# Hybrid block with 32 experts on one core: first weight piece cast by GpSimd in three transfers, scatter between gate and up, last product in bank 6

## The chip, the core and the metric

The kernel runs on one core of a Trainium2 chip. The core has TensorE (PE, with its weight loads as PEld), VectorE (DVE), ScalarE (ACT), GpSimd (POOL), SyncE (SP), which here does nothing but issue transfers, and 16 DMA engines. The metric is the device time of one execution in microseconds (us), lower is better.

## The reference, cut to what matters

One decoder block in float32 for 256 tokens of width 1024: a mixing part (window attention and a short convolution), then a mixture of 32 experts of which each token uses four. All 32 experts are computed, and each has three matrices of 1024 x 1024, so that 96 matrices of 4 MB (4.19 million bytes) must be read from HBM.

```
h = rms_norm(x, g_mix);  proj = h @ w_in + b_in
...
x = x + (sigmoid(ga) * y_attn + sigmoid(gc) * y_conv) @ w_out
h = rms_norm(x, g_ffn)
top_logit, top_idx = lax.top_k(h @ w_router + b_router, 4);  top_w = softmax(top_logit)
for each expert e, for the tokens sent to it:
    g = min(xb @ w_gate[e] + b_gate[e], 7);  u = clip(xb @ w_up[e] + b_up[e], -7, 7)
    y = (g * sigmoid(1.702 * g) * (u + 1)) @ w_down[e] + b_down[e]
    x[token] += top_w * y
out = rms_norm(x, g_final)
```

## The kernel before

The order of the work is written out by hand, engine by engine; semaphores join the engines, and nothing is scheduled by a planner.

**The first stage** (to about 250 us) is the mixing part. A float32 product is made there from a high part and a low rest: weights come in pieces of 128 x 2048 elements into one of three raw slots, a cast rounds them to the high part `wH`, and a subtraction gives the rest `wL`. The very first piece is special: `x` and the piece are the first transfers on SP's queue (line 344 and 347), the piece in two halves with the semaphores `first_in` and `piece_full[0]`. ScalarE casts its first quarter (`first_weights(0, 2)`, line 1045), VectorE the second (line 1297), GpSimd the second half (line 1662). Meanwhile PE runs `WARM` = 3 idle products on zeros (line 610, two instructions of the hardware for one), then transposes the normed `x` (line 587; VectorE makes it in eight quarter rows at line 1287); ScalarE and VectorE turn the transposes into `hH` and `hL` (lines 1049 and 1299), and PE starts `project_first` (line 600).

**The second stage** is the experts. An expert `j` has two slots ("runs") of 2 MB for gate, up and down each. All are streamed by SP through a ring of ten slots, in the order of use; from expert 5 on in whole matrices (lines 474 to 479, only the up matrix of every fifth expert in two parts), in the last two experts by slots (line 361). SP waits until PE has used the slot (`weights_used`) before it issues the next load into it. The last four slots (`HALVED`: LAST - 3 to LAST) land in two halves each, the very last in a half and two quarters (line 375).

PE does for each expert: the gate product (`wide(4, ...)`, line 831, bank 4, bias at line 797), the up product (bank 5), then `scatter(j, j)` (line 845), which adds the output of the expert before to the 256 tokens in banks 0 to 3, then `turn_act` (line 858) and `turn_weights` (line 852, into bank 4), then `gather(j + 1)` (line 761, bank 6), which fetches the next expert's tokens, and the down product (bank 7) with `turn_xe` (line 769) between its two slots. The down product waits for `aT_ready`, which ScalarE gives after copying the turned activations (`take_act`, line 1175). ScalarE also copies the gathered rows (`take_rows`, line 1143) and the finished output (`take_y`, line 1180), and VectorE does `swiglu`, `take_weights` (`S_ready`, line 1532) and `take_xe` (`xe_ready`, line 1545).

The experts 0 to 4 are written out, 5 to 29 are a loop over groups of five (`UNROLL`), and `last_pair` does 30 and 31 in an order of its own: gate 30, gather, up 30, `turn_xe`, scatter, the turns, gate 31, up 31, down 30, scatter, down 31, and a last scatter. Both down products there write bank 7, so that the scatter of 30 stands between them and waits for ScalarE's copy. The final norm and the output follow.

Of the kernel before, what the change touches and what calls it, by code (L numbers as in the profile page):

```python
# [27 lines left out]
P = 128  # L28
# [33 lines left out]
UNROLL = 5  # L62
FREED = (0, 1, 4)
LAST = NE * EP - 1
HALVED = (EP, *(RING + p for p in FREED), LAST - 3, LAST - 2, LAST - 1, LAST)
SSQ0 = 2 + 2 * NKV
RSTD0 = 4
WARM = 3
# [60 lines left out]
def hybrid_block(nc, A, out):  # L129
    ctx = ExitStack()  # L130
    with ctx:
# [128 lines left out]
        first_in, second_high, rest_high = sem("first_in"), sem("second_high"), sem("rest_high")  # L260
# [77 lines left out]
        def _(sp):  # L338
# [6 lines left out]
            for half, full in enumerate((first_in, piece_full[0])):  # L345
                ks = slice(4 * half, 4 * half + 4)
                sp.dma_start(raw_slot(0).rearrange("p (k n) -> p k n", k=KB)[:, ks],
                             w_in[:, ks, KCOL * PW:(KCOL + 1) * PW]).then_inc(full, 16)
# [164 lines left out]
        def _(pe):  # L513
# [286 lines left out]
            def wide(b, src, first_p, uses, bias_of, base=None, between=None, paired=False, by_halves=None):  # L800
# [3 lines left out]
                for run in range(RUNS):  # L804
# [14 lines left out]
                    for k2 in range(RUN):  # L819
                        if halved and base + p == LAST and k2 == RUN // 2:  # L820
                            pe.wait_ge(quarter_full, 16)
                        elif halved and k2 == (RUN - 1 if base + p == LAST else RUN // 2):
                            pe.wait_ge(slot_full[s], uses(p))
# [15 lines left out]
            def scatter(nth, chunk):  # L839
# [3 lines left out]
                for t in range(TT):  # L843
# [5 lines left out]
            def turn_weights(j):  # L849
                pe.wait_ge(Gw_ready, j + 1)  # L850
                for t in range(TT):
                    tr = pe.transpose(bank(4, t * P, P), Gw[:, t, :, :].rearrange("p h c -> p (h c)"), ident)  # L852
# [27 lines left out]
            def expert(j, c, uses, paired, up_halves):  # L880
# [26 lines left out]
                if not at(j, 0):  # L907
# [15 lines left out]
            def group(it, paired):  # L923
                for c in range(UNROLL):
                    expert(it * UNROLL + c, c, lambda p: (it - paired) * (16 * in_group) + 16 * (p // RING + 1), paired,
                           it * 16 if paired else None)

            def last_pair():
# [73 lines left out]
        def _(act_e):  # L1002
# [41 lines left out]
            act_e.wait_ge(first_in, 16)  # L1044
            nc.scalar.copy(*first_weights(0, 2)).then_inc(first_high, 1)
# [132 lines left out]
            def take_y(used):  # L1178
                act_e.wait_ge(weights_used, used)
                nc.scalar.copy(ysb, psum[:, 7, :]).then_inc(ysb_ready, 1)  # L1180
# [11 lines left out]
            for j in range(UNROLL):  # L1192
# [7 lines left out]
            with act_e.Fori(1, NE // UNROLL) as it:  # L1200
# [13 lines left out]
            take_y(NE * EP)  # L1214
# [23 lines left out]
        def _(dve):  # L1238
# [291 lines left out]
            def take_weights(j):  # L1530
                dve.wait_ge(S_turned, j + 1)
                v.tensor_copy(S, psum[:, 4, 0:256]).then_inc(S_ready, 1)  # L1532
# [39 lines left out]
            for j, used in ((NE - 2, (NE - 2) * EP), (NE - 1, (NE - 2) * EP + 2 * RUNS)):  # L1572
# [70 lines left out]
        def _(pool):  # L1643
# [16 lines left out]

            pool.wait_ge(piece_full[0], 16)
# [63 lines left out]
```

## Time and profile before

| what | us |
|---|---|
| median of 3 runs | 1163.14 (1162.24 to 1163.76) |
| the profiled execution, its own time | 1162.93 |
| its span in the profile | 1161.1 |
| PE busy in it | 1120.4 (97%) |
| 16 DMA engines busy, main queue | 92.9% of the span |

The profile's times count from the start of the span; 1.8 us of the execution lie around it. A busy PE includes modelled ends of pipelined products; a row's mean is the time of one instruction from its start to that end, so that steps are better read from starts.

### The profile page before, as it was taken

The page shows a single profiled execution, that of the slowest core. Times are in us where ns is not written, and L with a number is a line of the kernel's source. Part 1 is how long each engine was busy: PE and PEld are TensorE (multiplying, and loading weights), DVE is VectorE, ACT ScalarE, POOL GpSimd, SP SyncE. Part 2 cuts the span into 40 slices and gives each one's busy share as a digit, 9 for nine tenths or more (in the row PEclk, how much of TensorE's full clock was granted, in tenths as well). Part 3 has the DMA queues.
Part 4 walks back from the last instruction along what each step waited for, and adds up shares of the span by engine and source line. Part 5 has one row for each costly group of instructions (what it writes and reads, how often), then busy time and mean ns, then how long its engine had stood idle before and what let it go on. Part 6 is the DMA issues. An engine that isn't in the chain of part 4 may idle for free.

```text
span 1161.1 us, 14240 instructions
## 1 busy us (share of the span) xinstructions
PE 1120.4 (97%) x5623; PEld 522.9 (45%) x5623; DVE 359.9 (31%) x684; ACT 238.9 (21%) x426; POOL 26.9 (2%) x59
## 2 busy tenths in 40 slices
PE   8999999999999999999999999999999999999997
PEld 7888888973333333333333333333333333333332
DVE  6988897742111112112111111111111111111111
ACT  6676765421000000100010000000000000000002
POOL 2100000000000000000000000000000000000000
PEclk9999999999999999999999999999999999999999
DMA  9455749899999999999999999999999999999996
GB/s 295 157 175 169 263 143 350 298 407 428 428 427 434 427 430 432 427 432 430 430 432 430 435 433 432 432 426 433 429 432 433 427 437 433 432 430 424 430 423 244
DMA packets 62913, 447.44 MB, mean 385 GB/s; under 512 B 4649, under 2 KB 44933, under 8 KB 46501
## 3 DMA queue, kind: packets, MB, share of 16 engines
q1 hardware_dynamic: 62608, 446.93, 92.9%
q8 instruction: 20, 0.33, 0.1%
q10 hardware_dynamic: 277, 0.12, 0.0%
q14 instruction: 8, 0.07, 0.0%
HBM read 445.59 MB, written 1.05 MB: 385 GB/s over the span
## 4 chain that ended last, share of the span: by engine, by line
PE 75%; DMA 23%; ACT 0%; DVE 0%; issue 0%; POOL 0%; ACTq 0%; DVEq 0%; POOLq 0%
PE psum L831 42%; DMA ring<-in_w_up 20%; PE psum L540 10%; PE psum L544 5%; PE psum L845 4%; PE psum L761 4%; DMA ring<-in_w_down 3%; PE psum L560 2%; PE psum L769 1%; PE psum L858 1%; PE psum L797 1%; PE psum L610 0%; PE psum L852 0%; PE psum L600 0%; PE psum L526 0%; PE psum L874 0%
## 5 line engine op out<-in xcount | busy, mean ns | idle before, releaser
L831 PE MATMUL psum<-ring,work 128*64 128x512 f32 x3072 | 693.1, 601 | 27.0 <-DMA ring<-in_w_up 21.6
L831 PEld LDWEIGHTS psum<-ring,work 128*64 128x64 f32 x3072 | 217.6, 138 | 453.6 <-issue 406.0
L1522 DVE TENSOR_SCALAR work<-psum 128x512 f32<-128x512 f32 x32 | 22.1, 692 | 285.2 <-PE psum L831 285.2
L540 PE MATMUL psum<-hh,w 128*128 128x512 f32 x384 | 97.4, 395 | 0.0
L1266 DVE TENSOR_TENSOR w<-ring,w 128x1024 fp32r<-128x1024 f32 x74 | 90.4, 1264 | 8.6 <-ACT w L1015 8.3
L1527 DVE TENSOR_SCALAR work<-psum 128x512 f32<-128x512 f32 x32 | 22.1, 692 | 196.4 <-PE psum L831 196.4
L1175 ACT COPY work<-psum 128x512 f32<-128x512 f32 x32 | 18.8, 587 | 301.9 <-PE psum L858 301.8
L1015 ACT CAST w<-ring 128x1024 fp32r<-128x1024 f32 x74 | 74.2, 1049 | 28.3 <-PE psum L544 15.2
L1545 DVE TENSOR_TENSOR work<-psum,g2k 128x256 f32<-128x256 f32 x62 | 23.4, 419 | 168.7 <-PE psum L769 168.7
L540 PEld LDWEIGHTS psum<-hh,w 128*128 128x128 f32 x384 | 68.9, 189 | 15.0 <-ACT w L1015 1.3
L1184 ACT ACTIVATE work<-work 128x512 f32<-128x512 f32 x32 | 20.1, 630 | 230.4 <-DVE work L1522 230.4
L1180 ACT COPY work<-psum 128x512 f32<-128x512 f32 x32 | 18.8, 586 | 228.2 <-PE psum L831 228.2
L845 PE MATMUL psum<-work 64*128 64x512 f32 x256 | 63.6, 615 | 1.4 <-ACT work L1180 1.4
L761 PE MATMUL psum<-xres,work 128*64 128x512 f32 x248 | 61.5, 618 | 0.0
L544 PEld LDWEIGHTS psum<-hh,w 128*128 128x128 f32 x384 | 52.3, 190 | 3.8
L544 PE MATMUL psum<-hh,w 128*128 128x256 f32 x384 | 53.5, 282 | 0.0
L845 PEld LDWEIGHTS psum<-work 64*128 64x128 f32 x256 | 22.0, 186 | 41.9 <-issue 38.6
L1532 DVE COPY work<-psum 128x256 f32<-128x256 f32 x32 | 13.6, 425 | 56.2 <-PE psum L852 47.1
L1525 DVE TENSOR_TENSOR work<-work 128x512 f32<-128x512 f32 x32 | 22.2, 693 | 25.8 <-ACT work L1184 25.8
L1143 ACT COPY work<-psum 128x512 f32<-128x512 f32 x31 | 18.2, 586 | 52.4 <-PE psum L761 52.4
L858 PEld LDWEIGHTS psum<-cst,work 128*128 128x128 f32 x128 | 17.9, 209 | 24.4 <-DVE work L1528 22.0
L769 PEld LDWEIGHTS psum<-cst,work 128*128 128x128 f32 x124 | 17.3, 209 | 25.2 <-issue 25.2
(210 smaller groups left out, 688.5 us busy)
## 6 DMA issues: line engine op xcount, KB each, us to landing
ring<-in_w_gate SPq DMA_DIRECT2D x25, 4096.0 KB, 39.5
ring<-in_w_down SPq DMA_DIRECT2D x25, 4096.0 KB, 39.7
ring<-in_w_up SPq DMA_DIRECT2D x20, 4096.0 KB, 37.1
ring<-in_w_up SPq DMA_DIRECT2D x23, 2048.0 KB, 35.5
ring<-in_w_gate SPq DMA_DIRECT2D x13, 2048.0 KB, 13.1
ring<-in_w_in SPq DMA_DIRECT2D x25, 1024.0 KB, 5.1
ring<-in_w_down SPq DMA_DIRECT2D x8, 2048.0 KB, 13.3
ring<-in_w_down SPq DMA_DIRECT2D x10, 1024.0 KB, 37.4
```

The lines of the kernel that those rows point to most:

```text
L540: pe.matmul(bank(b[m]).rearrange("p (x t) -> p x t", x=2), wH[:, par, m, k, :], both[:, :, k, :], start=(k == 0), stop=(k == KB - 1))
L544: mm = pe.matmul(bank(b[m], 0, T), wL[:, par, m, k, :], both[:, 0, k, :], start=False, stop=(k == KB - 1), skip_group_check=True)
L560: mm = pe.matmul(bank(b[t], t * PW, PW).rearrange("p (m n) -> p m n", m=2), x[:, k, t * P:(t + 1) * P], w[:, par, :, k, :], start=(k == 0 ...
L761: mm = pe.matmul(psum[64 * h:64 * h + 64, 6, :].rearrange("p (i r) -> p i r", r=RUN), Gr[:, t, :], x_runs[:, :, h, :], start=(t == 0), sto ...
L769: tr = pe.transpose(bank(6, r * P, P), rows.rearrange("p (i r) -> p i r", r=RUN)[:, :, r], ident)
L831: mm = pe.matmul(to, src[:, k, :], moving, start=(bias_of is None and k == 0), stop=(k == KB - 1), tile_position=(0, 64 * h))
L845: pe.matmul(bank(2 * t + h), S[64 * h:64 * h + 64, t * P:(t + 1) * P], ysb[64 * h:64 * h + 64, :], start=False, stop=False, skip_group_che ...
L858: tr = pe.transpose(bank(5, b * P, P), act_runs[:, b // RUN, :, b % RUN], ident)
L1015: nc.scalar.copy(wH[:, par, m, :, :], raw_slot(s).rearrange("p (k n) -> p k n", k=KB)[:, :, m * P:(m + 1) * P],).then_inc(wH_ready, rise i ...
L1266: v.tensor_tensor(wL[:, par, m, :, :], raw_slot(s).rearrange("p (k n) -> p k n", k=KB)[:, :, m * P:(m + 1) * P], wH[:, par, m, :, :].bitca ...
L1525: steps.link(v.tensor_tensor(gm, gm, sg, ALU.mult))
L1545: ins = v.tensor_tensor(to, turned, gain.unsqueeze(2).broadcast_to([P, RUN, CW]), ALU.mult)
```

## The change

Three edits. First, the first weight piece comes in three transfers (a quarter, a quarter, a half), all three parts are cast by GpSimd, and `WARM` is 2. Second, from expert 10 on (`BACKLOG` = 2 groups of five are written out now) PE scatters the expert before between the gate and the up product, and gathers for the next one ahead of the turns; ScalarE copies the gathered rows ahead of the activations. Third, in the last pair: VectorE takes the next expert's tokens ahead of the scatter weights, which stand in bank 7 instead of 4 for expert 30; the wait on `S_ready` moves from ahead of gate 31 to ahead of down 30; the last down product writes bank 6 and has the scatter of expert 30 in its middle; and slot LAST - 4 lands in halves too.

```diff
+BACKLOG = 2
-HALVED = (EP, *(RING + p for p in FREED), LAST - 3, LAST - 2, LAST - 1, LAST)
+HALVED = (EP, *(RING + p for p in FREED), LAST - 4, LAST - 3, LAST - 2, LAST - 1, LAST)
-WARM = 3
+WARM = 2
@@ sync
-            for half, full in enumerate((first_in, piece_full[0])):
-                ks = slice(4 * half, 4 * half + 4)
+            for k0, k1, full in ((0, 2, first_in), (2, 4, second_in), (4, KB, piece_full[0])):
+                ks = slice(k0, k1)
@@ tensor, wide()
                     for k2 in range(RUN):
+                        if middle is not None and run == 0 and k2 == RUN // 2:
+                            middle()
@@ tensor, expert()
+                if caught_up:
+                    scatter(j, j)
                 wide(5, xe, c * EP + RUNS, uses, 1, base, None, paired, up_halves if c == UNROLL - 1 else None)
                 if at(j, 0):
                     pe.wait_ge(wT_ready, 1)
+                if at(j, 0) or caught_up:
                     gather(j + 1)
                 else:
                     scatter(j, j)
...
-                if not at(j, 0):
+                if not (at(j, 0) or caught_up):
                     gather(j + 1)
@@ tensor, last_pair()
-                turn_weights(a)
+                turn_weights(a, 7)
                 pe.wait_ge(xe_ready, b + 1)
                 pe.wait_ge(picked, b + 1)
-                pe.wait_ge(S_ready, b)
                 wide(4, xe, 2 * RUNS, uses, 0, base)
...
+                pe.wait_ge(S_ready, b)
                 wide(7, aT, 4 * RUNS, uses, None, base, turn_last)
-                scatter(b, b)
                 pe.wait_ge(aT_ready, b + 1)
-                wide(7, aT_last, 5 * RUNS, uses, None, base)
-            group(0, False)
-            with pe.Fori(1, NE // UNROLL) as it:
-                group(it, True)
+                wide(6, aT_last, 5 * RUNS, uses, None, base, middle=lambda: scatter(b, b))
+            for it in range(BACKLOG):
+                group(it, it > 0, False)
+            with pe.Fori(BACKLOG, NE // UNROLL) as it:
+                group(it, True, True)
@@ scalar
-            act_e.wait_ge(first_in, 16)
-            nc.scalar.copy(*first_weights(0, 2)).then_inc(first_high, 1)
...
+                    take_rows(j + 1)
                     take_act(j)
-                    take_rows(j + 1)
...
-            take_y(NE * EP)
+            act_e.wait_ge(scattered, 4 * NE)
+            take_y(NE * EP, 6)
@@ vector
-                if k == 2:
-                    dve.wait_ge(first_in, 16)
-                    v.tensor_copy(*first_weights(2, 4)).then_inc(second_high, 1)
...
-                if j == NE - 1:
-                    dve.wait_ge(scattered, 4 * NE)
-                take_weights(j)
                 if j < NE - 1:
                     take_xe(j + 1)
+                    take_weights(j, 7)
+                else:
+                    dve.wait_ge(scattered, 4 * NE)
+                    take_weights(j)
@@ gpsimd
+            pool.wait_ge(first_in, 16)
+            g.tensor_copy(*first_weights(0, 2)).then_inc(first_high, 1)
+            pool.wait_ge(second_in, 16)
+            g.tensor_copy(*first_weights(2, 4)).then_inc(second_high, 1)
             pool.wait_ge(piece_full[0], 16)
             g.tensor_copy(*first_weights(4, 8)).then_inc(rest_high, 1)
```

PE's program for one expert of the loop, before; L797 is the bias, L831 the products (16 stand for one matrix), L845 the scatter, L858 and L852 the turns of activations and weights, L761 the gather, L769 the turn of the next tokens:

```order
L797 MATMUL psum<-bias,chosen 64x512 x2
L831 MATMUL psum<-ring,work 64x512 x16
L797 MATMUL psum<-bias,chosen 64x512 x2
L831 MATMUL psum<-ring,work 64x512 x16
L845 MATMUL psum<-work 128x512 x4
L858 MATMUL psum<-cst,work 128x128 x4
L852 MATMUL psum<-cst,work 128x128 x2
L757 REGISTER_ALU
L761 MATMUL psum<-xres,work 64x512 x4
L831 MATMUL psum<-ring,work 64x512 x8
L769 MATMUL psum<-cst,work 128x128 x4
L831 MATMUL psum<-ring,work 64x512 x8
```

And in the changed kernel, where the line numbers are up to 3 higher (L834 products, L848 scatter, L861 and L855 turns, L762 gather):

```order
L798 MATMUL psum<-bias,chosen 64x512 x2
L834 MATMUL psum<-ring,work 64x512 x16
L848 MATMUL psum<-work 128x512 x4
L798 MATMUL psum<-bias,chosen 64x512 x2
L834 MATMUL psum<-ring,work 64x512 x16
L758 REGISTER_ALU
L762 MATMUL psum<-xres,work 64x512 x4
L861 MATMUL psum<-cst,work 128x128 x4
L855 MATMUL psum<-cst,work 128x128 x2
L834 MATMUL psum<-ring,work 64x512 x8
L770 MATMUL psum<-cst,work 128x128 x4
L834 MATMUL psum<-ring,work 64x512 x8
```

The scatter moved ahead of the up product's bias, and the gather took its place ahead of the turns; between the turns and the down product nothing is left.

PE's program at the end of the last pair before, from the bias of gate 31 on:

```order
L797 MATMUL psum<-bias,chosen 64x512 x2
L831 MATMUL psum<-ring,work 64x512 x16
L797 MATMUL psum<-bias,chosen 64x512 x2
L831 MATMUL psum<-ring,work 64x512 x24
L858 MATMUL psum<-cst,work 128x128 x4
L852 MATMUL psum<-cst,work 128x128 x2
L831 MATMUL psum<-ring,work 64x512 x8
L845 MATMUL psum<-work 128x512 x4
L831 MATMUL psum<-ring,work 64x512 x16
L845 MATMUL psum<-work 128x512 x4
```

And in the changed kernel:

```order
L798 MATMUL psum<-bias,chosen 64x512 x2
L834 MATMUL psum<-ring,work 64x512 x16
L798 MATMUL psum<-bias,chosen 64x512 x2
L834 MATMUL psum<-ring,work 64x512 x24
L861 MATMUL psum<-cst,work 128x128 x4
L855 MATMUL psum<-cst,work 128x128 x2
L834 MATMUL psum<-ring,work 64x512 x12
L848 MATMUL psum<-work 128x512 x4
L834 MATMUL psum<-ring,work 64x512 x12
L848 MATMUL psum<-work 128x512 x4
```

The first of the two scatters moved four products back, into the middle of the first slot of the last down product.

## Rows read from the trace of the kernel before

**Rows 1.** The page: PE's share of the span; the DMA engines' busy tenths in 40 slices.

```profile
PE 1120.4 (97%) x5623; PEld 522.9 (45%) x5623; DVE 359.9 (31%) x684; ACT 238.9 (21%) x426; POOL 26.9 (2%) x59
...
DMA  9455749899999999999999999999999999999996
```

**Rows 2.** Stretches: length, busy us of PE PEld DVE ACT POOL, granted clock, DMA share, GB/s.

```profile
16.50:244.00 227.50, 227.50 (x1453) 201.20 (x1452) 184.99 (x268) 143.82 (x262) 10.47 (x13) 1.00 0.69 235
500.00:630.00 130.00, 130.00 (x618) 46.31 (x614) 22.82 (x49) 11.95 (x20) 1.17 (x5) 1.00 1.00 432
634.00:1050.00 416.00, 390.81 (x1798) 135.50 (x1794) 69.39 (x155) 34.19 (x58) 3.28 (x14) 0.98 1.00 432
1051.30:1060.10 8.80, 8.73 (x34) 2.63 (x34) 0.00 (x0) 0.00 (x0) 0.00 (x0) 0.81 0.99 425
```

**Rows 3.** Chain that ended last: start us, length us, what; the last DMA in it.

```profile
1014.30 37.03 DMA ring<-in_w_up
```

**Rows 4.** Three of the last loads, each: issue (ns, us) and us to landing.

```profile
L375 SPq DMA_DIRECT2D ring<-in_w_down x1: 2062/2062/2062, 1099.8 to 1099.8; - x1
...
DMA to landing us min/median/max: 39.5/39.5/39.5
...
L375 SPq DMA_DIRECT2D ring<-in_w_down x1: 12155/12155/12155, 1103.2 to 1103.2; - x1
...
DMA to landing us min/median/max: 41.1/41.1/41.1
...
L375 SPq DMA_DIRECT2D ring<-in_w_down x1: 3321/3321/3321, 1124.0 to 1124.0; - x1
...
DMA to landing us min/median/max: 25.8/25.8/25.8
```

**Rows 5.** Timeline of the last experts: start us, length us, instruction, idle before.

```profile
1051.37 8.78 PE L831 MATMUL psum<-ring,work 128*64 128x512 f32 x32 [2.36 <-DMA ring<-in_w_up]
...
1086.66 1.99 PE L845 MATMUL psum<-work 64*128 64x512 f32 x8
...
1088.58 0.75 PE L858 MATMUL psum<-cst,work 128*128 128x128 f32 x4
...
1089.36 0.59 ACT L1175 COPY work<-psum 128x512 f32<-128x512 f32 x1 [8.33 <-PE psum L858]
...
1089.47 1.94 PE L761 MATMUL psum<-xres,work 128*64 128x512 f32 x8
...
1119.70 0.42 PE L797 MATMUL psum<-bias,chosen 96*64 96x512 bf16 x2 [1.18 <-DVE work L1545]
...
1142.68 1.99 PE L845 MATMUL psum<-work 64*128 64x512 f32 x8 [0.69 <-ACT work L1180]
...
1144.60 7.09 PE L831 MATMUL psum<-ring,work 128*64 128x512 f32 x32
```

**Rows 6.** Timeline of the first microseconds.

```profile
2.63 5.30 PE L610 MATMUL psum<-ring 128*128 128x512 f32 x6 [2.63 <-POOL ring L1646]
...
8.01 1.97 PE L587 MATMUL psum<-cst,normed 128*128 128x128 f32 x16
...
8.20 1.13 DVE L1287 TENSOR_SCALAR normed<-xres,small 128x256 f32<-128x256 f32 x4
...
9.32 3.03 ACT L1049 ACTIVATE hh<-psum,parT 128x256 fp32r<-128x256 f32 x8 [0.75 <-PE psum L587]
...
9.49 1.04 POOL L1662 CAST w<-ring 128x1024 fp32r<-128x1024 f32 x1 [1.48 <-DMA ring<-in_w_in]
...
10.50 4.22 PE L600 MATMUL psum<-hh,w 128*128 128x256 f32 x32 [0.45 <-issue]
...
11.04 2.44 DVE L1299 SCALAR_TENSOR_TENSOR hh<-psum,parT,hh 128x256 fp32r<-128x256 f32 x6
```

**Rows 7.** Groups by form: busy us, mean ns; the idle products and the same shape later.

```profile
L610 PE MATMUL psum<-ring 128*128 128x512 f32 x6 | 5.3, 1054 | 2.6 <-POOL ring L1646 2.6
...
L743 PE MATMUL psum<-xres,cst 128*128 128x512 f32 x8 | 3.9, 616 | 0.0
```

More of the change, by code:

```diff
@@ L259, in hybrid_block @@
         quarter_full, quarter_used = sem("quarter_full"), sem("quarter_used")
-        first_in, second_high, rest_high = sem("first_in"), sem("second_high"), sem("rest_high")
+        first_in, second_in, second_high, rest_high = sem("first_in"), sem("second_in"), sem("second_high"), sem("rest_high")
         x_in = [sem(f"x_in{t}") for t in range(TT)]
@@ L798, in add_bias, with wide @@
                               columns(bias3[:, bias_of, :], h), start=True, stop=False, tile_position=(0, 64 * h))
-            def wide(b, src, first_p, uses, bias_of, base=None, between=None, paired=False, by_halves=None):
+            def wide(b, src, first_p, uses, bias_of, base=None, between=None, paired=False, by_halves=None, middle=None):
                 if bias_of is not None and not (base == 0 and first_p == 0):
@@ L837, in wide, with scatter @@
                     mm.then_inc(weights_used, 1)
-            def scatter(nth, chunk):
+            def scatter(nth, chunk, ts=range(TT)):
                 pe.wait_ge(ysb_ready, chunk)
                 pe.wait_ge(S_ready, chunk)
-                for t in range(TT):
+                for t in ts:
                     for h in range(2):
@@ L847, in scatter, with turn_weights @@
                                   tile_position=(64 * h, 0)).then_inc(scattered, 1)
-            def turn_weights(j):
+            def turn_weights(j, b=4):
                 pe.wait_ge(Gw_ready, j + 1)
                 for t in range(TT):
-                    tr = pe.transpose(bank(4, t * P, P), Gw[:, t, :, :].rearrange("p h c -> p (h c)"), ident)
+                    tr = pe.transpose(bank(b, t * P, P), Gw[:, t, :, :].rearrange("p h c -> p (h c)"), ident)
                 tr.then_inc(S_turned, 1)
@@ L878, in at, with expert @@
                 return isinstance(j, int) and j == n
-            def expert(j, c, uses, paired, up_halves):
+            def expert(j, c, uses, paired, up_halves, caught_up):
                 base = (j - c) * EP if isinstance(j, int) else None
@@ L921, in _, with group @@
             in_group = UNROLL * EP // RING
-            def group(it, paired):
+            def group(it, paired, caught_up):
                 for c in range(UNROLL):
                     expert(it * UNROLL + c, c, lambda p: (it - paired) * (16 * in_group) + 16 * (p // RING + 1), paired,
-                           it * 16 if paired else None)
+                           it * 16 if paired else None, caught_up)
             def last_pair():
@@ L1176, in take_act, with take_y @@
                                psum[:, 5, :].rearrange("p (b h c) -> p b h c", b=4, h=2)).then_inc(aT_ready, 1)
-            def take_y(used):
+            def take_y(used, b=7):
                 act_e.wait_ge(weights_used, used)
-                nc.scalar.copy(ysb, psum[:, 7, :]).then_inc(ysb_ready, 1)
+                nc.scalar.copy(ysb, psum[:, b, :]).then_inc(ysb_ready, 1)
             def squash(j):
@@ L1191, in _ @@
             nc.scalar.copy(wT[:, :], psum[0:NE, 6, 0:256]).then_inc(wT_ready, 1)
-            for j in range(UNROLL):
+            for j in range(BACKLOG * UNROLL):
                 squash(j)
@@ L1199, in _ @@
                 take_y((j + 1) * EP)
-            with act_e.Fori(1, NE // UNROLL) as it:
+            with act_e.Fori(BACKLOG, NE // UNROLL) as it:
                 for c in range(UNROLL):
@@ L1528, in swiglu, with take_weights @@
                 v.scalar_tensor_tensor(act, uc, 1.0, gm, ALU.add, ALU.mult).then_inc(act_ready, 1)
-            def take_weights(j):
+            def take_weights(j, b=4):
                 dve.wait_ge(S_turned, j + 1)
-                v.tensor_copy(S, psum[:, 4, 0:256]).then_inc(S_ready, 1)
+                v.tensor_copy(S, psum[:, b, 0:256]).then_inc(S_ready, 1)
             def gained(hs):
```

## The prediction

> **What bounds the kernel now.** I began with the page. PE is busy for 97% of the span, which looks like a kernel bound by PE; but the DMA engines, too, stand at nine tenths from slice 10 on [rows 1]. So two engines are near their limits, and the stretches say which one gives the time. From 500 to 630 us PE passes 618 products without idling; an expert of this order has 126 (96 of weights, 8 scatter, 8 gather, 4 bias, 10 turns), so it takes 126 x 130 / 618 = 26.5 us [rows 2]. From 634 to 1050 us it passes 1798 in 416 us, 29.15 us an expert, and idles for 25 us, while the transfers run at 432 GB/s and a DMA share of 1.00 in both stretches [rows 2]. One matrix is 4.19 MB, so it lands every 9.71 us and three take 29.1 us: from about 630 us on the weights set the pace. Before that PE was slower than it could be only because the ring still held a stock, which it ate up at 2.6 us an expert.
>
> Two things follow. The transfers are saturated from about slice 8 on, so nothing that PE does in the middle moves their end; it moves only if the whole stream starts earlier. And what remains is the end, after the last time that PE waited for a transfer. The chain gives it: an up matrix issued at 1014.30 lands 37.03 us later, at 1051.33 [rows 3]. From there PE works without another wait for weights to 1144.60 + 7.09 = 1151.69, the end of the last product, which is 9.4 us ahead of the span's end; of other waits in that time there are 1.18 and 0.69 us [rows 5]. Did PE then fall behind the transfers? The last quarter of the last slot is issued at 1124.0 and lands after 25.8 us, at 1149.8 [rows 4]. PE takes the last two slots from 1144.60, so 3.43 us each to the next start, and comes to that quarter three quarters into the second slot, at 1150.7. So PE is later than the weights by 0.9 us and no more. That is the most that a better order of PE can give there, unless the stream itself comes earlier.
>
> **The change part by part, by the chain's end first: the scatter between gate and up.** In the changed rows an expert has the same instructions; what is new is which of them lie ahead of a wait. For experts 10 to about 14, where PE sets its own pace, the order costs something. The scatter (1.92 us from its start at 1086.66 to the next at 1088.58) used to cover VectorE's work behind the up product; the gather (1.77 us to the next start) takes that place and covers it about as well. But the gather used to cover ScalarE's copy of the turned activations, too. That copy starts at 1089.36, 0.78 us behind the turns, and takes 0.59 [rows 5], so it is ready 1.4 us behind their start, while the two turns take 0.89 (1088.58 to 1089.47) [rows 5]. So PE now waits 0.5 to 0.55 us ahead of each down product. ScalarE's new order (rows first) does not add to it, since its 0.6 us copy of the rows runs beside the turns. At 26.5 + 0.55 = 27.1 us PE is still faster than the transfers' 29.1, so it only meets them later, and the stream doesn't notice: cost nothing, because the 2 us an expert that it lacks to the pace of the transfers cover it.
>
> From about 650 us on, PE used to idle at up matrices and then scatter; now it scatters first. At the wait at 1051.37 it had idled for 2.36 us, and the two slots behind it took 8.78 us [rows 5] where 6.9 are usual, with a granted clock of 0.81 in that stretch [rows 2], that is part of it at the lower of the two levels, 1.2 GHz. The wait becomes shorter by the 1.92 us of the scatter, some 0.5 us remain, and the 1.9 us of slow clock should go too. From 1051.4 on I step PE through, with each matrix landing 9.71 us after the one before:
> - up 28 ends at 1058.3, gather and turns and the wait to 1061.5, down to 1069.2 (before: 1072.4). Then gate 29 waits for its landing at 1051.3 + 19.4 = 1070.8.
> - gate 29 to 1077.7, scatter, up 29 (1.9 + 0.2 + 6.9) to 1086.7, gather to 1088.5. Down 29 lands at 1090.2 and PE starts it there; before it started at 1089.47 + 1.77 = 1091.2.
>
> So of 3.2 us that the new order wins after the last wait, 0.9 are left two matrices later: the weights are in the way again. **The last pair:** up 30 ends 0.9 us earlier, and gate 31, which waited 1.18 us for `take_xe` [rows 5], no longer does. In its place comes `picked`, GpSimd's choice of the bias, which I put at 0.3 us of wait. Gate 31 then starts 1.8 us earlier, at 1118.1, and up 31 at 1125.2, both a little behind their landings. Then the pieces of 1 MB: the second half of down 30's second slot lands at 1099.8 + 39.5 = 1139.3 and the second half of down 31's first at 1103.2 + 41.1 = 1144.3 [rows 4], the ones around them 2.5 us apart. PE takes the former's 8 products from 1139.4 to 1141.1, waits for the first half of down 31 (1141.8), works to 1143.6, scatters for 1.9, then does one slot and a half: 1145.5 + 1.7 + 3.4 = 1150.7. The copy of bank 7, for which the scatter waited 0.69 us [rows 5], lies under the half slot. The last product ends at 1150.9 against 1151.7: **-0.8 us**. Splitting slot LAST - 4 lets up 31 pass that slot without a wait (its first half lands 2.5 us sooner); nothing is on the path for it.
>
> **The head.** The idle products end at 2.63 + 5.30 = 7.93 and the transposes start at 8.01 [rows 6]; with two instead of three the idle ones end at 6.2. But then VectorE is in the way: it makes the second token tile's quarters from 8.20 on, 0.28 us each [rows 6], and ScalarE's first `hH`, which needs the transpose of the first of them, starts at 9.32. That quarter is ready at about 8.5, its transpose was the ninth of sixteen, at 8.01 + 8 x 0.11 = 8.9. Now it can follow at 8.55. So the chain to PE's first product (10.50 [rows 6]) moves by 0.35 to 0.45 us. VectorE loses its cast (0.42 us), but it lay in a gap: the six products that follow it start at 11.04 [rows 6] because `hH` was not there yet. GpSimd has the two new casts, half of 1.04 us each [rows 6], between 8.05 and 9.3, and the third starts at 9.49 as before, because its data comes then. Everything that PE needs is cast a microsecond ahead. The third transfer costs SP 0.5 us more issue time, while its engines are busy with what is queued (the piece needed next comes by bandwidth, not by issue). From 16.5 to 244 us PE is busy for all of 227.5 us [rows 2], so the shift reaches the point where SP gets ring slots, and with it the stream: **-0.4 us** for all that follows.
>
> What speaks against this: VectorE's eight quarters (0.28 us for 256 columns each [rows 6]) now lie beside GpSimd's casts. If each cast held VectorE up for its 0.52 us, the second tile's first quarter would come at 9.0 instead of 8.5, `hH` at 9.4 instead of 9.32, and the head would win nothing or lose 0.1. No row shows such a block, so I keep -0.4 and take that for a rival. The Trainium skill, "SBUF — State Buffer", section "Who interferes with whom", states it as a rule: VectorE in a two-port mode and GpSimd hold one pair of ports exclusively, and the other blocks for the whole instruction. By that rule the sum would lose its -0.4.
>
> Sum on the profiled execution: 1162.93 - 0.8 - 0.4 = 1161.7. Its time lies 0.2 under the median of the three runs, so by that median 1163.14 - 1.2 = **1161.9 us**, 0.10% less. A measurement of this kernel tells no less than about 0.2%, 2.3 us, from no change.
>
> **The rivals.**
> - *The head gives nothing*, because the casts hold VectorE up as priced above, or by the clock. The idle products take 5.3 / 6 = 0.88 us each, the same shape later 3.9 / 8 = 0.49 [rows 7]: they run at the low level of 1.2 GHz, and the transposes behind them, 0.11 us apart, no longer. With one less and an idle half microsecond ahead of the first transposes the higher clock may come later. The stretch at 1051 us lost 8.78 - 6.9 = 1.9 us to it [rows 5]; the same here gives -1.2 + 1.9 = +0.7. So 1162.3 to 1163.9. The Trainium skill, "TensorE: Matmul & The Clock Gate", part 1, says that the throttled state is the default and that activity releases it, which fits that row. Chance 0.16.
> - *PE wins its full idle product* (1.77 us) at the head, because the quarters are not what holds it. The stream moves with it, and the end by at most 0.9 more: 1163.1 - 2.7 = 1160.4. Against it stands the start of the quarters at 8.20 after the first tile's. Chance 0.07.
> - *The wait ahead of the down product becomes the bound*, on the other side. It decides from 29.15 - 26.5 = 2.6 us an expert. If turns, both copies and VectorE's work stood one behind the other (0.7 + 0.6 + 0.6 + 1.4 = 3.3 us), an expert would take 29.8 us, twenty of them from 520 us on would end at 1116 instead of 1099, and the time would be 1180. The rows show the copies beside PE's work, not behind it [rows 5]. Chance 0.03.
> - *The new order wins nothing at the end*: PE's lead is used up between the landings, because the last pieces come some tenths later than I read them or a turn or a `picked` waits longer than I put it; the 0.8 us are only the difference of two such chains. Then -0.4 alone is left, 1162.7. Chance 0.12.
>
> **How the numbers follow.** The forecast, 1161.2 to 1162.6, has 0.57; 0.05 is left for what I don't see, half on each side. The range that holds 8 in 10 reaches from between the second rival and the forecast to the top of the first, 1160.6 to 1163.9. Faster by over 0.2% needs 1160.8 or less: the second rival, the lower edge of the forecast and the unseen, 0.11. Slower by over 0.2% needs 1165.5: the third rival and the unseen, 0.06. The rest, 0.83, is no change.
>
> **What would show it.** The first `hH` near 8.95 and PE's first product near 10.1; two idle products and transposes 0.11 us apart. In the loop a wait of 0.5 us ahead of each down product, released by ScalarE; waits for up matrices under 1 us where 2.36 were, and no granted clock under 1 there. Landings still 9.71 us apart, the last near 1149.4. The last product's end near 1150.5, with its last wait for a weight quarter. I would be wrong if the rate of the transfers changed, since 1% of it is 9 us, or if the stream had gaps behind the first experts that the earlier start closes or opens.

## The result, and the profile after

| | median us | runs |
|---|---|---|
| before | 1162.36 (1161.36 to 1164.53) | 22 |
| changed kernel | 1164.27 (1162.78 to 1168.41) | 22 |

The ratio is 1.0019, with a 95% interval of 1.0013 to 1.0024: the change costs 2.2 us (1.5 to 2.8). The forecast was 1161.9, and 1164.27 lies above the top of the range, 1163.9. The forecast stood on the median of three runs, 1163.14, which is 0.8 us above the median of 22; as a difference, -1.2 was forecast and +2.2 came. The profiled execution took 1165.37 us, with a span of 1163.2 (before 1162.93 and 1161.1).

The page of the changed kernel, for [rows 1], and its stretches, for the third of [rows 2]:

```profile
PE 1118.3 (96%) x5621; PEld 520.8 (45%) x5621; DVE 360.9 (31%) x683; ACT 238.0 (20%) x425; POOL 27.9 (2%) x61
...
DMA  9455749899999999999999999999999999999996
...
q8 instruction: 25, 0.41, 0.1%
...
634.00:1050.00 416.00, 390.74 (x1820) 134.67 (x1818) 70.42 (x160) 33.99 (x57) 3.26 (x14) 1.00 1.00 432
```

PE is busy 2.1 us less and its clock is full in the long stretch, where it was 0.98; the transfers run at the same 432 GB/s. PE gained, and the span grew nonetheless. One row differs, the loads of instructions: 25 here, and in the page of before 20:

```profile
q8 instruction: 20, 0.33, 0.1%
```

The timeline of the first microseconds, for [rows 6]:

```profile
8.56 0.63 POOL L1665 CAST w<-ring 128x512 fp32r<-128x512 f32 x1
...
8.79 2.46 DVE L1292 TENSOR_SCALAR normed<-xres,small 128x256 f32<-128x256 f32 x4
9.14 0.67 POOL L1667 CAST w<-ring 128x512 fp32r<-128x512 f32 x1
...
10.21 3.02 ACT L1053 ACTIVATE hh<-psum,parT 128x256 fp32r<-128x256 f32 x8 [3.41 <-PE psum L588]
...
11.05 0.70 PE L588 MATMUL psum<-cst,normed 128*128 128x128 f32 x4 [0.30 <-DVE normed L1292]
...
11.75 2.03 PE L601 MATMUL psum<-hh,w 128*128 128x256 f32 x15
```

VectorE's four quarters beside the casts take 2.46 us where they took 1.13, and PE's first product starts at 11.75 instead of 10.50. (0.6 us of that was there before the casts, at the quarters' start of 8.79 against 8.20; where the quarters start differs from execution to execution, so the length is the reading.)

The last experts on PE, for [rows 5]:

```profile
1043.92 7.09 PE L834 MATMUL psum<-ring,work 128*64 128x512 f32 x32 [1.12 <-DMA ring<-in_w_gate]
...
1053.63 7.09 PE L834 MATMUL psum<-ring,work 128*64 128x512 f32 x32 [0.37 <-DMA ring<-in_w_up]
...
1063.79 3.65 PE L834 MATMUL psum<-ring,work 128*64 128x512 f32 x16 [0.46 <-ACT work L1179]
...
1120.29 0.42 PE L798 MATMUL psum<-bias,chosen 96*64 96x512 bf16 x2 [0.32 <-POOL chosen L1693]
...
1144.41 1.94 PE L834 MATMUL psum<-ring,work 128*64 128x512 f32 x8 [0.64 <-DMA ring<-in_w_down]
1146.28 1.99 PE L848 MATMUL psum<-work 64*128 64x512 f32 x8
1148.20 5.57 PE L834 MATMUL psum<-ring,work 128*64 128x512 f32 x24
1154.51 1.99 PE L848 MATMUL psum<-work 64*128 64x512 f32 x8 [0.74 <-ACT work L1184]
```

The waits are about those that were forecast: 0.46 ahead of the down product, 0.37 for the up matrix where 2.36 was, 0.32 for `picked`. Yet the last product ends at 1148.20 + 5.57 = 1153.77 instead of 1151.69. The landings say why. The last two quarters of the weights, with their time from issue to landing:

```profile
L376 SPq DMA_DIRECT2D ring<-in_w_down x2: 2106/2122/2137, 1124.8 to 1126.9; - x2
...
DMA to landing us min/median/max: 25.6/26.1/26.5
```

The last lands 25.6 us behind 1126.9, at 1152.6; before it was 1149.8 [rows 4]. So the end of the stream moved by 2.8 us, and PE follows it more closely (1.2 us instead of 1.9). The stream's beginning moved by 1.1 of these: the first expert's up matrix is issued at 215.5 here and lands 7.5 us later, at 223.1, and landed at 222.0 before. The other 1.7 us arise within the stream, where I had said that nothing could.

### The profile page after: what moved, and what is told of

It reads as the page before. It is cut to its first block, busy times and chain, and to the rows that moved or that the text cites. A ratio compares the mean times of both kernels' runs of the same rounds, so it can differ in the third digit from the quotient of the medians.

```text
span 1163.2 us, 14215 instructions
## 1 busy us (share of the span) xinstructions
PE 1118.3 (96%) x5621; PEld 520.8 (45%) x5621; DVE 360.9 (31%) x683; ACT 238.0 (20%) x425; POOL 27.9 (2%) x61
## 4 chain that ended last, share of the span: by engine, by line
PE 63%; DMA 35%; ACT 1%; DVE 0%; issue 0%; ACTq 0%; POOL 0%; SPq 0%; DVEq 0%
PE psum L834 34%; DMA ring<-in_w_down 13%; DMA ring<-in_w_gate 11%; DMA ring<-in_w_up 10%; PE psum L541 10%; PE psum L545 5%; PE psum L762 3%; PE psum L848 3%; PE psum L561 2%; PE psum L770 1%; PE psum L861 1%; PE psum L798 1%; DMA cst<-in_constants 0%; PE psum L877 0%; PE psum L601 0%; PE psum L527 0%
## 5 line engine op out<-in xcount | busy, mean ns | idle before, releaser
L834 PE MATMUL psum<-ring,work 128*64 128x512 f32 x3072 | 685.9, 595 | 31.7 <-DMA ring<-in_w_gate 15.5
L834 PEld LDWEIGHTS psum<-ring,work 128*64 128x64 f32 x3072 | 213.9, 137 | 439.5 <-issue 380.6
L848 PE MATMUL psum<-work 64*128 64x512 f32 x256 | 63.6, 615 | 0.7 <-ACT work L1184 0.7
L762 PE MATMUL psum<-xres,work 128*64 128x512 f32 x248 | 60.6, 611 | 0.0
L848 PEld LDWEIGHTS psum<-work 64*128 64x128 f32 x256 | 22.0, 186 | 41.2 <-issue 39.4
L762 PEld LDWEIGHTS psum<-xres,work 128*64 128x64 f32 x248 | 17.2, 139 | 32.7 <-issue 32.7
L861 PEld LDWEIGHTS psum<-cst,work 128*128 128x128 f32 x128 | 18.0, 209 | 25.9 <-DVE work L1530 23.1
```

Of the source, the lines that this page charges most:

```text
L762: mm = pe.matmul(psum[64 * h:64 * h + 64, 6, :].rearrange("p (i r) -> p i r", r=RUN), Gr[:, t, :], x_runs[:, :, h, :], start=(t == 0), sto ...
L834: mm = pe.matmul(to, src[:, k, :], moving, start=(bias_of is None and k == 0), stop=(k == KB - 1), tile_position=(0, 64 * h))
L848: pe.matmul(bank(2 * t + h), S[64 * h:64 * h + 64, t * P:(t + 1) * P], ysb[64 * h:64 * h + 64, :], start=False, stop=False, skip_group_che ...
L861: tr = pe.transpose(bank(5, b * P, P), act_runs[:, b // RUN, :, b % RUN], ident)
```

## The experiments

Each kernel was timed in 11 runs, beside 33 of the kernel before that the kernels of one series share. An interval is about 0.09% wide on either side, 1.0 us, so that a single part of the change stands at the edge of what can be told; a difference given in us is the ratio's. A profile shows one execution.

**Series 1: the head and the order apart.** `e1_head_all` is the whole head of the change (three transfers, casts by GpSimd, two idle products) with the old order; `e2_casts` has the transfers and the casts with three idle products; `e3_warm2` has the two idle products alone; `e4_order` is the changed kernel with the head of before.

```diff
# e1, e2 (e1 also WARM = 2)
+            pool.wait_ge(first_in, 16)
+            g.tensor_copy(*first_weights(0, 2)).then_inc(first_high, 1)
+            pool.wait_ge(second_in, 16)
+            g.tensor_copy(*first_weights(2, 4)).then_inc(second_high, 1)
# e1, e2: the casts of ScalarE and VectorE go, the third transfer is that of e16
# e3
-WARM = 3
+WARM = 2
# e4: the change without these, ScalarE and VectorE cast as before
```

> The kernel before with all of the head of the change (three transfers, all casts on GpSimd, two idle products), order untouched. Theory 1, the head costs the time: the profile of the changed kernel has PE's first product at 11.75 instead of 10.50 us and all landings about 1.1 us later, so +1.0 to +1.3 us. Rival, the head is neutral and the order behind it costs the 2 us: within 0.3 us of before.

Measured: 1163.11 against 1161.98, ratio 1.0014 (1.0004 to 1.0023), +1.6 us.

> The kernel before with three transfers and all casts on GpSimd, but three idle products. Theory 1a, GpSimd's casts hold VectorE up: the second tile's four quarter rows take 2.4 us instead of 1.13 and the time is +0.6 to +1.2 us. Rival 1b, the missing idle product costs the time by a later clock: the quarters take 1.1 us and the time is -0.4 to +0.1.

Measured: 1162.87, ratio 1.0008 (0.9999 to 1.0017), +0.9 us.

> The kernel before with two idle products and nothing else. Theory 1a: transposes start near 7.0 us, the first product moves by -0.3 to 0 us, so the time is -0.3 to +0.1. Rival 1b: the granted clock rises only near 11 us, the transposes stand 0.2 us apart and the time is +0.5 to +1.0.

Measured: 1162.35, ratio 1.0001 (0.9992 to 1.0010).

> The changed kernel with the head of before (two transfers, casts on three engines, three idle products). If the head is the only loss, the order keeps what the prediction gave it at the end, -0.8 us to before. If the order itself has a price (the stream of weights is delayed in the middle, where the changed profile shows landings another 1.2 us later than the head explains), +0.5 to +1.2 us.

Measured: 1162.96, ratio 1.0006 (0.9997 to 1.0015), +0.7 us. The timeline of the head of `e2_casts`:

```profile
7.88 0.63 POOL L1657 CAST w<-ring 128x512 fp32r<-128x512 f32 x1
...
8.11 2.48 DVE L1285 TENSOR_SCALAR normed<-xres,small 128x256 f32<-128x256 f32 x4
8.45 0.67 POOL L1659 CAST w<-ring 128x512 fp32r<-128x512 f32 x1
...
9.40 1.04 POOL L1661 CAST w<-ring 128x1024 fp32r<-128x1024 f32 x1 [0.27 <-DMA ring<-in_w_in]
...
10.51 3.21 DVE L1294 SCALAR_TENSOR_TENSOR hh<-psum,parT,hh 128x256 fp32r<-128x256 f32 x8
...
11.08 2.75 PE L600 MATMUL psum<-hh,w 128*128 128x256 f32 x21
```

The four quarters start in time, at 8.11, and are stretched by 1.35 us. The second and the fourth of them by themselves, where 0.35 us is the length of one that nothing disturbs:

```profile
8.57 0.70 DVE L1285 TENSOR_SCALAR normed<-xres,small 128x256 f32<-128x256 f32 x1
...
9.45 1.13 DVE L1285 TENSOR_SCALAR normed<-xres,small 128x256 f32<-128x256 f32 x1
```

The second ends at 9.27, 0.15 us behind the end of the second cast (9.12), and the fourth at 10.58, 0.14 behind the end of the third (10.44). So the two new casts hold VectorE up for 0.2 and 0.35 us, and that is enough for the last quarter to meet the third cast, the half piece that GpSimd had before too: it costs the most, 0.78 us. In the kernel before, that cast started at 9.49, when the quarters were through. `hL` on the same engine (line 1294) then starts only at 10.51, and PE's first product waits for that. So by `e1_head_all` the head costs 1.6 us (0.5 to 2.7); the casts alone point the same way, but their interval reaches zero. In the times of `e3_warm2` the idle product shows no cost, and in its trace PE's first product starts 2.2 us behind the start of the second tile's quarters, where 2.3 were before. The order, which was to win 0.8, shows no gain either and points the other way.

**Series 2: what of the order costs.** `e5_written_out` only writes experts 5 to 9 out, in the old order; `e6_pair` has only the new last pair; `e7_loop` has the new order in the loop with the old pair and head; `e8_late_bias` is `e4_order` with PE's spreading of the down bias (the `spread_down_bias` call) moved from expert 4 to expert 9, away from the point near 397 us where SP issues late.

```diff
# e5 (PE; ScalarE's loop likewise)
+            for it in range(BACKLOG):          # BACKLOG = 2
+                group(it, it > 0, False)
+            with pe.Fori(BACKLOG, NE // UNROLL) as it:
+                group(it, True, False)
# e6: BACKLOG = 1, nothing caught up, the new last_pair
# e7: group(it, True, True) in the loop, the old last_pair
# e8
-                if at(j, UNROLL - 1):
+                if at(j, 2 * UNROLL - 1):
                     spread_down_bias()
```

> The kernel before, with the experts 5 to 9 written out on PE and ScalarE instead of looped and nothing else; the order of every engine's work stays as it was. Theory 2a, the order's loss is the price of more program: five more 16 KB code loads lie beside the weights, each keeps one DMA engine for about 1 us, and the stream is up to 1 us longer: +0.3 to +1.0 us. Rival 2b, it comes from the order itself: within 0.3 us of before.

Measured: 1163.22 against 1162.02, ratio 1.0010 (1.0001 to 1.0019), +1.2 us.

> The kernel before with the last pair of the change alone (bank 6, scatter in the middle, bank 7 for the weights, LAST - 4 in halves); loop order and head of before. The prediction's step for the end: gate 31 no longer waits 1.18 us, the second scatter no longer 0.69, and PE's last product ends 0.6 to 0.9 us nearer the last landing (1.89 us behind it before), so -0.5 to -0.9 us. Rival: the stream's own end moves later as in the two profiles with this tail, where one 1 MB piece took 3.3 to 3.5 us instead of 2.5, and the time is within 0.3 us of before.

Measured: 1161.97, ratio 1.0000 (0.9991 to 1.0009).

> The changed kernel's loop order (written-out experts 5 to 9, scatter between gate and up from expert 10 on) with the head and the last pair of before. Theory 2a: the reorder wins nothing where the stream sets the pace and the code loads remain, +0.2 to +1.0 us. Rival 2b, the new wait ahead of each down product costs at the end: more than +1 us. By the prediction's sum the end is the last pair's, so -0.3 to 0.

Measured: 1163.04, ratio 1.0007 (0.9998 to 1.0016), +0.8 us.

> The kernel of e4 (order and last pair of the change, head of before), with the down bias (8 products of 32 rows, 3.6 us, followed by the low clock at 383 us) moved from expert 4 to expert 9. Theory 3, the stream has one tight place: at about 397 us SP issues a matrix only 1.9 to 5.4 us ahead of the end of the one in flight, and when PE is late there the stream stops for 0.2 to 1.8 us. With the bias later that issue comes 5 us earlier, the stretch of three matrices takes 29.1 us in every profile, and the time is 0.4 to 1.0 us below e4's. Rival: the stream never stops there and the time is e4's within 0.3 us.

Measured: 1162.45, ratio 1.0004 (0.9995 to 1.0013), +0.5 us, which can't be told from the +0.7 of `e4_order`. The kernel with nothing new but five experts written out is as slow as the whole order: it executes the same instructions on the same data. What differs is where its code comes from. Transfers from 520 to 1100 us, of the kernel before, the changed one, and, from series 3, the one with ten experts more written out:

```profile
q1 hardware_dynamic: 9357, 250.16, 100.3%
```

```profile
q1 hardware_dynamic: 9309, 250.01, 100.3%
q8 instruction: 5, 0.08, 0.1%
```

```profile
q1 hardware_dynamic: 9336, 249.71, 100.2%
q8 instruction: 10, 0.16, 0.1%
```

In this stretch the kernel before, whose loop is running, loads no code, and each expert more that is written out brings one load of 16 KB (0.08 MB in five) into a stream that fills the engines.

**Series 3: the two suspects undone.** `e9b_order_looped` is `e4_order` with `BACKLOG` = 1 (the new order already from expert 5, no more code than before); `e10b_written_more` is `e5_written_out` with 3; `e11b_head_wait` is `e1_head_all` with GpSimd's casts kept behind VectorE's quarters; `e12b_all_mended` is the changed kernel with both mends.

```diff
# e9b, e12b
-BACKLOG = 2
+BACKLOG = 1
# e10b
-BACKLOG = 2
+BACKLOG = 3
# e11b, e12b
+            pool.wait_ge(normed_ready, 4 * TT)
             pool.wait_ge(first_in, 16)
             g.tensor_copy(*first_weights(0, 2)).then_inc(first_high, 1)
```

> The kernel of e4 (order and last pair of the change, head of before) with the experts 5 to 9 in the loop again, in the new order too (BACKLOG = 1). Theory 4, what the order costs is the written-out program: 20 code loads instead of 25, the stream from its first expert landing to its last back from 928.8 to about 927.4 us, and the time 0.8 to 1.5 us below e4's, so -0.8 to -0.2 against before. Rival 4b, the order of the work costs it: e4's time within 0.3 us.

Measured: 1162.23 against 1162.24, ratio 0.9999 (0.9990 to 1.0009).

> The kernel of e5 (order of before) with the experts 10 to 14 written out as well, so 30 code loads. Theory 4a, each load costs alike: another +0.8 to +1.3 us, +2.0 to +2.5 against before. Theory 4b, loads cost only where they meet an engine that is late already: anything from +1.2 to +2.5. Rival, the number of loads is not the cause: within 0.3 us of e5, or of before.

Measured: 1163.90, ratio 1.0014 (1.0005 to 1.0023), +1.6 us.

> The kernel of e1 (whole head of the change, order of before), with GpSimd's first cast waiting until VectorE has made all eight quarter rows. Theory 1a, the casts held VectorE up: the second tile's quarters take 1.13 us again instead of 2.47, ScalarE starts on hH near 8.9, PE's first product comes near 10.2 instead of 10.8 and the time is 0.6 to 1.6 us below e1's, so -0.4 to +0.4 against before. Rival, the third transfer or the later clock is what costs: e1's time within 0.3 us.

Measured: 1162.56, ratio 1.0002 (0.9993 to 1.0011), +0.2 us where `e1_head_all` had +1.6.

> The changed kernel with both mendings: GpSimd's casts wait for VectorE's quarters, and the experts 5 to 9 are in the loop (BACKLOG = 1). If the causes are the two that I hold them for, the prediction's own sum for the change should come out, -1.2 to -0.4 us against before; if another part of the change costs, it stays above before.

Measured: 1162.11, ratio 1.0000 (0.9991 to 1.0009). The head of `e11b_head_wait`:

```profile
8.27 1.14 DVE L1285 TENSOR_SCALAR normed<-xres,small 128x256 f32<-128x256 f32 x4
...
9.48 0.61 POOL L1658 CAST w<-ring 128x512 fp32r<-128x512 f32 x1 [1.24 <-DVE normed L1285]
9.71 3.45 DVE L1294 SCALAR_TENSOR_TENSOR hh<-psum,parT,hh 128x256 fp32r<-128x256 f32 x8 [0.30 <-ACT hh L1047]
...
10.30 3.50 PE L600 MATMUL psum<-hh,w 128*128 128x256 f32 x27 [0.31 <-DVE hh L1294]
```

With one wait more on GpSimd the quarters are back to 1.14 us, and PE's first product starts 2.03 us behind their start instead of 2.97 (`e2_casts`: 11.08 - 8.11). It is 2.96 or 2.97 in all three kernels with the early casts, 2.0 to 2.5 in the twelve that cast as before, and 2.0, 2.0 and 2.7 in the three with the wait (`e11b`, `e12b`, `e15_mended_bias` of series 4). That settles where the head's block comes from.

Writing out costs: +1.2 us for five experts more and +1.6 for ten (`e5` and `e10b`), both clear of zero. But the step from five to ten lies within the interval, so that a price for each load is not shown. The new order with no more code than before shows no cost. The traces tell more than the times here. From the landing of the first expert's up matrix (near 222 us) to the last landing of all, the stream takes 926.2 to 929.1 us, 927.3 in the mean, in the twelve profiles with 20 loads; 928.3 to 929.5, 928.8 in the mean, in the five with 25; and 928.5 in the one with 30. So the kernels with more written out have a stream about 1.5 us longer, two of the twelve others reach it as well (`e2_casts` 928.4, `e12b_all_mended` 929.1), and in the one trace with five loads more on top they add nothing.

Both mends together bring the changed kernel to the time of the one before, within 1 us, and no further: the -1.2 to -0.4 that I expected of them doesn't show.

**Series 4: a third suspect, and the transfers.** In several profiles SP issues an up matrix near 390 us so late that the stream nearly stops. In the changed kernel:

```profile
L480 SPq DMA_DIRECT2D ring<-in_w_up x1: 333/333/333, 397.2 to 397.2; - x1
...
DMA to landing us min/median/max: 13.0/13.0/13.0
```

The matrix queued ahead of it lands at 399.1, so that only 1.9 us of transfers were queued (3.5 us in the kernel before), and the stretch from 376 to 410 us ran at 409 GB/s in place of 425:

```profile
376.00:410.00 34.00, 34.00 (x140) 12.08 (x138) 4.91 (x11) 2.39 (x4) 0.23 (x1) 0.90 0.97 409
```

`e13_bias_end` is the kernel before with the spreading of the down bias behind the down product of expert 4, `e14_looped_bias` is `e9b` with that, `e15_mended_bias` `e12b` with that. `e16_transfers` has the three transfers of the head alone.

```diff
# e13, e14, e15
-                if at(j, UNROLL - 1):
-                    spread_down_bias()
                 turn_act(j)
...
+                if at(j, UNROLL - 1):
+                    spread_down_bias()
# e16
-            for half, full in enumerate((first_in, piece_full[0])):
+            for k0, k1, full in ((0, 2, first_in), (2, 4, second_in), (4, KB, piece_full[0])):
```

> The kernel before with the down bias of expert 4 (3.6 us of PE, and the low clock behind it) moved from ahead of that expert's down product to behind it, so that SP gets the slots of the down product 3.6 to 5 us earlier. Theory 3, the stream stops at the tight place near 397 us when PE is late there: three matrices take 29.1 us in the profile instead of 29.3 to 30.3, and the time is -0.2 to -1.2 us. Rival: the stream loses nothing there on average, within 0.2 us of before.

Measured: 1161.89 against 1161.93, ratio 0.9998 (0.9989 to 1.0007).

> The kernel of e9 (order and last pair of the change looped from expert 5 on, head of before), with the down bias moved as in e13. If theory 3 holds the gain adds to e9's: -1.5 to -0.5 us against before, which would beat both kernels. Rival: e9's time, within 0.3 us of before.

Measured: 1162.32, ratio 1.0002 (0.9993 to 1.0011).

> The kernel of e12 (whole change, GpSimd's casts behind VectorE's quarters, looped from expert 5 on), with the down bias moved as in e13. Its profile had the largest loss at the tight place (31.4 us for three matrices instead of 29.1), so here the move should show most: 29.1 us there and -1.8 to -0.6 us against before. Rival: e12's time, within 0.3 us of before.

Measured: 1162.53, ratio 1.0005 (0.9996 to 1.0014).

> The kernel before with the first piece in three transfers, the casts on ScalarE, VectorE and GpSimd as before, three idle products. Theory 1a, the casts alone cost at the head: quarters of the second tile in 1.13 us, PE's first product at 10.5 +-0.3, the time within 0.3 us of before. Rival 1c, the third transfer delays the constants and the pieces behind it: +0.4 to +0.9 us.

Measured: 1162.14, ratio 1.0001 (0.9992 to 1.0010). The stretch in `e13_bias_end`:

```profile
376.00:410.00 34.00, 34.00 (x146) 11.73 (x142) 6.29 (x13) 2.38 (x4) 0.23 (x1) 0.95 1.01 432
```

The edit did what it should: 432 GB/s where the kernel before has 425, and the issue came 5.6 us earlier (388.9 instead of 394.5). The time did not follow, with -0.2, +0.2 and +0.6 us in three kernels. That theory of mine fell: what is lost there in a profile isn't seen as a cost in the times, where 1 us can be told. In `e16_transfers` the quarters take 1.13 us, as before.

## Why the prediction was wrong

**The head, -0.4 us, failed.** The step was: "If each cast held VectorE up for its 0.52 us, the second tile's first quarter would come at 9.0 instead of 8.5, `hH` at 9.4 instead of 9.32, and the head would win nothing or lose 0.1. No row shows such a block, so I keep -0.4". The block is there, and longer than I priced: the two casts take 0.63 and 0.67 us, and VectorE's four quarters take 2.48 us instead of 1.13. A quarter that meets a cast that is under way ends 0.14 to 0.15 us behind that cast. By the Trainium skill, "SBUF — State Buffer", section "Who interferes with whom", that is what should happen, and trace and measurement agree with it; the missing row would have been an argument only if before had had a cast of GpSimd beside these quarters. The size was wrong as well, for two reasons. I priced only the two new casts, which cost the quarters 0.55 us together, and took the third as harmless because it starts "as before"; but quarters that are late by that much run into it, for another 0.78 us. And I followed the stall only to `hH` on ScalarE, which isn't late at all (9.14 in `e2_casts`, 9.32 before). What is late next is VectorE's own `hL` (10.51 behind the quarters in `e2_casts`, 9.71 in `e11b_head_wait`), and PE's first product needs both. The measured term is +0.9 (`e2`) to +1.6 us (`e1`), each within 1 us. Two idle products instead of three (`e3`, +0.1) and the third transfer (`e16`, +0.1) are neutral, as far as 1 us can be told. A later rise of the clock, my other condition for this rival, is not what costs: `e3_warm2` tests the idle product alone, with PE's first product no later behind the quarters than before.

**"The stream doesn't notice" failed.** The step was: "The transfers are saturated from about slice 8 on, so nothing that PE does in the middle moves their end; it moves only if the whole stream starts earlier." PE indeed moved nothing. But the edit also wrote five experts out, and I counted that at nothing: I asked what instructions do and not where they come from. The time is +1.2 us for the writing out alone, +0.7, +0.8 and +0.5 in the kernels with the new order too (`e4`, `e7`, `e8`), +1.6 for twice as much, and -0.1 without it; the six kernels that cast as before and have no more code lie between -0.2 and +0.2. That writing out costs is shown, by these times and by the longer streams; that it acts through the loads of code beside the stream is my reading. The load in 1147.5 to 1149 us of the changed kernel takes 4.4% of 16 engines' time, 1.06 us of one engine. Five such loads spread evenly over 16 engines would be 0.3 us (an estimate from that row); how they become a microsecond and more may be seen at the stream's end. Stretches of the last landings of the changed kernel (columns as in [rows 2]):

```profile
1142.00:1146.00 4.00, 3.36 (x16) 0.89 (x14) 0.00 (x0) 0.58 (x1) 0.00 (x0) 1.00 1.00 417
1146.80:1150.10 3.30, 3.30 (x16) 0.87 (x12) 0.42 (x1) 0.00 (x0) 0.00 (x0) 1.00 0.68 268
1150.10:1152.57 2.47, 2.47 (x14) 0.77 (x12) 0.00 (x0) 0.00 (x0) 0.00 (x0) 1.00 0.14 56
```

And the last stretch of the kernel before:

```profile
1147.30:1149.80 2.50, 2.50 (x14) 0.79 (x12) 0.00 (x0) 0.00 (x0) 0.00 (x0) 1.00 0.11 38
```

In the last 2.47 us a share of 0.14, some 2 of 16 engines, is all that works, and before it was 0.11: the engines don't finish together, with or without the extra loads. If the last landing is set by the engine that has most left, a code load on that one counts in full, and on another not at all. That reading fits that the cost is not proportional (5 loads 1.2, 10 loads 1.6, and no longer stream in the trace with 30). It is argued, not shown: the records that I read don't say which engine a load of code took, and which loads cost stays open.

**The end, -0.8 us, was right in its waits and doesn't show in the times.** The waits came as forecast, to about 0.1 us. Left alone, in `e9b_order_looped`, the order gives this end:

```profile
1117.73 0.42 PE L798 MATMUL psum<-bias,chosen 96*64 96x512 bf16 x2 [0.32 <-POOL chosen L1694]
...
1141.71 1.94 PE L834 MATMUL psum<-ring,work 128*64 128x512 f32 x8 [0.64 <-DMA ring<-in_w_down]
1143.58 1.99 PE L848 MATMUL psum<-work 64*128 64x512 f32 x8
1145.50 5.37 PE L834 MATMUL psum<-ring,work 128*64 128x512 f32 x24
```

The last product ends at 1150.87, and 1150.9 was forecast. But its last weights landed at 1149.02 and not at 1149.8, so that PE stands 1.85 us behind them, against 1.89 before. That the last product ends where I had put it is luck: the weights were 0.8 us early. PE is closer to the landings (1.2 us) in the changed kernel, `e4_order` and `e8_late_bias`, and not in `e12b_all_mended` (1.9), whose last landing is as late (1150.6); why stays open. In the times the order is worth -0.1 us (`e9b`) and the new pair alone 0.0 (`e6`), each within 1 us. The forecast took the difference of two chains with the landings fixed; they vary by as much as it was worth.

**The sum.** The head by itself gives 0.9 to 1.6 us and the order with its written out code 0.7, together 1.6 to 2.3, and 2.2 was measured; each of these parts is known to 1 us only, so the agreement is no proof. The firmer one is that the kernel with both undone is back at 0.0 (`e12b`). The chances: part of the result's cause was in the first rival, "the head gives nothing", whose 1163.9 was its top; it lacked the second cause, for which no rival stood.

## What to carry to other kernels

Before GpSimd is given work beside VectorE, price the block for the full length of the instruction, look whether the delayed work now meets an instruction that it used to miss, and follow the stall to the next thing that the blocked engine itself has to do, not only to its first reader. When a kernel is bound by its transfers, give writing a loop out a price of its own: here five experts cost 1.2 us (0.1 to 2.2), which the order of instructions doesn't show. And a forecast of a part of a microsecond at the end of a stream needs the spread of the last landing, not one trace of it: with the same number of loads, the stream's length differed by 2.9 us over twelve traces.

## What the runs showed of the hardware

- VectorE's normalisation of 128 x 256 float32 (a tensor by a scalar for each partition, 0.35 us alone, 0.26 us from start to start) stood still while a cast of GpSimd that had started before it ran (128 x 512 float32 0.63 and 0.67 us, 128 x 1024 1.04 to 1.11): it ended 0.14 to 0.15 us behind the cast. Four took 1.13 us alone, 2.46 to 2.48 in three kernels, and 1.14 with the wait.
- Beside a saturated stream of weights (432 GB/s), 0, 5 and 10 code loads of 16 KB between 520 and 1100 us went with 0, 1.2 and 1.6 us, each to 1 us, and with streams of 927.3, 928.8 and 928.5 us from the first expert's landing to the last. That the loads themselves do it is not shown.
- In the last 2.5 us of the stream the share of busy DMA engines was 0.14 in the changed kernel and 0.11 in the one before: the 16 engines don't finish a stream together.
